# Two-layer streaming encoder on one core: another order for the first units of the frames' attention, both copies of summed outputs on ScalarE, and two layers joined without a barrier

## The chip, the core and the metric

The kernel runs on one core of one Trainium2 chip. The metric is device time in microseconds (us). A profiled execution gives a trace as well, with a span from its first to its last instruction. The engines are TensorE (PE, matmuls; its weight loads are PEld), VectorE (DVE), ScalarE (ACT), GpSimd (POOL) and SyncE (SP, which issues DMA transfers). Each engine works through its own list of instructions in order. The lists meet only in semaphores: a `wait_ge` holds the engine, and all that stands behind it on that engine, until another engine has counted a semaphore up.

## The reference: what is computed

1168 tokens (1024 prompt frames, 8 sample streams of 16 tokens, 16 meta tokens) pass through an input LayerNorm and two layers of

```
z = h @ w_in                                    # to latents, rotary key, window q, k, v
q, q_lat, q_rope, ckv, kr, sq, sk, sv           # RMS norms, rotary embeddings
o_lat = softmax(q_lat @ ckv' + q_rope @ kr') @ ckv        # 8 heads over latents, chunk causal
o_swa = softmax([sq @ sk', sink])[:-1] @ sv               # 8 heads over a window, learned sinks
x   = layer_norm(ALPHA * h + rms(o_lat @ w_uv, o_swa) @ w_out)
h   = layer_norm(ALPHA * x + (silu(x @ wg) * (x @ wu)) @ wd)
```

The outputs are h after layer 2, and each layer's new keys and values. All of it is float32; the kernel splits every operand into a high and a low part and multiplies three times, so that each product is three matmuls (lines 2403 to 2405).

## The kernel before

A layer has four phases. **A** (lines 2411 to 2494 on PE) takes the ten tiles of 128 tokens one by one: transpose the tile (`x_T`), multiply by `w_in` in three blocks (`z`), normalise and rotate on DVE, transpose keys and queries (`post`). **B** (line 2500 on) is the attention of the prompt's frames. **C** is the sample streams and the output projection. **D** is the feed-forward part, with its down projection, the transposes back (`y_T`) and the closing LayerNorm.

Between A and B, between B and C, and between the end of D and the next layer's A stands `barrier` (line 551): each of the five engines drains, counts `phase_done` up and waits for all five. `phase_no` numbers them.

**B's order is a list, `FRAMES`.** `plan_frames` (line 130) writes it, and PE, ACT and DVE each run through the same list, doing their part of each unit (`frames_pe`, `frames_hi`, `frames_lo`). The units are: `wk` turns the key weights; `kn` makes a pair of heads' keys, `vh` its values, `qn` its queries; `qr` makes the rotary queries of four tiles (s = 0 or 1), on DVE six products and a sum; `qs` and `qt` split and turn them; `sx` finds a window tile's score maxima (DVE `tensor_reduce` L2051), `sc` and `sm` turn those into a shift; `mx`, `mc`, `mt` do the same for the latent scores. Then `st` is one step of transposed scores, whose exponential ACT takes (L1558), `sp` splits the exponentials (DVE L2080 and L2084 for the even head, POOL L1262 for the odd), `pv` multiplies by the values into two banks of sums. A pass is a window tile (two steps) or four tiles of latent attention (five or nine). After a pass's last `pv`, `ox` copies the two banks of sums to `oT`: the even head on ACT (L1565), the odd on DVE (L2091). PE waits for both at the first `pv` of the next pass, since the banks are written anew, and at `ot`, which turns `oT`.

A unit's PSUM comes from a ring of three slots of two banks: unit i may start on PE only when unit i-3 of the ring has been read by ACT and DVE (`free_slot`).

Before B's first units DVE waits for ten small loads (`params`, line 1956), among them the meta values of `VB`; PE's keys of `kn` need DVE's `wukNl` behind that wait.

**The joint of the layers.** At D's end PE turns ten tiles back (`y_T`), DVE takes each one's statistics and its first product (`last_stats`, L2369), POOL the root, ACT and POOL or DVE the rest (`last_norm`, L2377 on DVE for tiles 7 and 9), POOL stores it. The next layer's `w_in` is split meanwhile: rows 5 to 7 early, rows 0 to 4 late, ACT making the high and DVE the low part (L608), all five of DVE's behind its last `last_norm`. Then the barrier; then PE turns tiles 0 and 1 (`x_T`, L2420), and starts `z`.

## Time and profile before

| | us |
|---|---|
| runs | 3321.43, 3327.38, 3342.14 (median 3327.38) |
| profiled execution, own time | 3323.12 |
| its span | 3320.8 |
| PE busy | 3074.2 (93%) |
| DVE / ACT / POOL busy | 1526.8 / 869.8 / 832.9 |
| mean granted TensorE clock | 0.959 of full speed |

Busy shares are of the span, and averages over phases with different limits. In a timeline row the number in brackets is how long the engine stood idle before the instruction, and what ended that. Phase B runs from about 201 to 540 us in layer 0 and from about 1845 to 2185 us in layer 1; the layers meet at about 1659 to 1681 us.

### The profile page before, as it was taken

The page shows a single profiled execution, that of the slowest core. Times are in us where ns is not written, and L with a number is a line of the kernel's source. Part 1 is how long each engine was busy: PE and PEld are TensorE (multiplying, and loading weights), DVE is VectorE, ACT ScalarE, POOL GpSimd, SP SyncE. Part 2 cuts the span into 40 slices and gives each one's busy share as a digit, 9 for nine tenths or more (in the row PEclk, how much of TensorE's full clock was granted, in tenths as well). Part 3 has the DMA queues.
Part 4 walks back from the last instruction along what each step waited for, and adds up shares of the span by engine and source line. Part 5 has one row for each costly group of instructions (what it writes and reads, how often), then busy time and mean ns, then how long its engine had stood idle before and what let it go on. Part 6 is the DMA issues. An engine that isn't in the chain of part 4 may idle for free. (4 is left out here: it accounts for less than half of the span.)

```text
span 3320.8 us, 46210 instructions
## 1 busy us (share of the span) xinstructions
PE 3074.2 (93%) x18240; PEld 2791.8 (84%) x18240; DVE 1526.8 (46%) x2883; ACT 869.8 (26%) x1678; POOL 832.9 (25%) x680
## 2 busy tenths in 40 slices
PE   7968888998999999999879788889999999999997
PEld 6956666877999999999879566668789999999996
DVE  6757777653222222222544677776532222222225
ACT  3333334435111111111223233344441111111111
POOL 2323333431212121111422233334212121111113
PEclk9989998999999999999989898989999999999998
DMA  4321104533111111110222211055331111111101
GB/s 161 129 78 34 33 23 153 167 124 110 45 38 42 40 44 38 38 38 25 109 97 98 69 33 33 23 159 178 110 110 42 41 43 39 38 38 38 38 25 71
DMA packets 129041, 231.68 MB, mean 70 GB/s; under 512 B 37744, under 2 KB 78960, under 8 KB 128592
## 3 DMA queue, kind: packets, MB, share of 16 engines
q1 hardware_dynamic: 118336, 198.80, 18.3%
q0 software_dynamic: 10576, 31.14, 2.4%
q8 instruction: 83, 1.36, 0.2%
q14 instruction: 46, 0.38, 0.0%
HBM read 175.46 MB, written 50.38 MB: 68 GB/s over the span
## 5 line engine op out<-in xcount | busy, mean ns | idle before, releaser
L2403 PE MATMUL PS<-xh,fwh 128*128 128x390 f32 (+1 forms) x2112 | 718.8, 340 | 2.0 <-DVE fwl L2309 1.4
L2404 PE MATMUL PS<-xl,fwh 128*128 128x390 f32 (+1 forms) x2112 | 720.0, 341 | 0.0
L2405 PE MATMUL PS<-xh,fwl 128*128 128x390 f32 (+1 forms) x2112 | 718.9, 340 | 0.0
L2351 DVE TENSOR_TENSOR acc<-acc,PS 128x390 f32<-128x390 f32 (+1 forms) x432 | 241.9, 560 | 420.6 <-PE PS L2405 420.6
L2329 DVE TENSOR_TENSOR gate<-PS,gate 128x390 f32<-128x390 f32 x132 | 74.4, 564 | 738.2 <-PE PS L2405 736.9
L2403 PEld LDWEIGHTS PS<-xh,fwh 128*128 128x128 f32 x2112 | 397.9, 188 | 5.1 <-DVE xl L2249 2.6
L2404 PEld LDWEIGHTS PS<-xl,fwh 128*128 128x128 f32 x2112 | 397.3, 188 | 0.4
L2405 PEld LDWEIGHTS PS<-xh,fwl 128*128 128x128 f32 x2112 | 397.3, 188 | 0.0
L2403 PE MATMUL PS<-hidh,fwh 128*128 128x390 f32 (+1 forms) x1056 | 359.5, 340 | 5.2 <-DVE hidl L2333 4.5
L2405 PE MATMUL PS<-hidh,fwl 128*128 128x390 f32 (+1 forms) x1056 | 360.8, 342 | 0.0
L2404 PE MATMUL PS<-hidl,fwh 128*128 128x390 f32 (+1 forms) x1056 | 359.4, 340 | 0.0
L1317 POOL TENSOR_TENSOR fwl<-raw,fwh 128x1024 fp32r<-128x1024 f32 x82 | 195.8, 2398 | 544.5 <-ACT fwh L1757 447.1
L1262 POOL TENSOR_TENSOR Pl<-Pf,Ph 128x256 fp32r<-128x256 f32 (+5 forms) x174 | 219.3, 1267 | 446.1 <-DVE Ph L2080 446.1
L1745 ACT ACTIVATE hidh<-gate 128x390 fp32r<-128x390 f32 x132 | 70.0, 531 | 989.3 <-DVE gate L2329 989.3
L1317 POOL TENSOR_TENSOR fwl<-fraw,fwh 128x1024 fp32r<-128x1024 f32 x42 | 100.4, 2391 | 773.6 <-ACT fwh L1762 673.2
L1558 ACT ACTIVATE Pf<-PS 128x512 f32<-128x512 f32 (+5 forms) x174 | 127.5, 751 | 321.1 <-PE PS L2509 320.8
L2403 PEld LDWEIGHTS PS<-hidh,fwh 128*128 128x128 f32 x1056 | 199.2, 189 | 6.4 <-issue 5.0
L2405 PEld LDWEIGHTS PS<-hidh,fwl 128*128 128x128 f32 x1056 | 200.2, 190 | 0.0
L2404 PEld LDWEIGHTS PS<-hidl,fwh 128*128 128x128 f32 x1056 | 199.0, 188 | 0.0
L2403 PE MATMUL PS<-winh,xTh 128*128 128x394 f32 (+3 forms) x480 | 171.4, 357 | 6.2 <-DVE xTl L1823 3.2
L2404 PE MATMUL PS<-winl,xTh 128*128 128x394 f32 (+3 forms) x480 | 167.5, 349 | 0.0
L2405 PE MATMUL PS<-winh,xTl 128*128 128x394 f32 (+3 forms) x480 | 167.0, 348 | 0.0
(441 smaller groups left out, 5421.1 us busy)
## 6 DMA issues: line engine op xcount, KB each, us to landing
raw<-in_W_FF SPq DMA_DIRECT2D x88, 512.0 KB, 3.2
fraw<-in_W_FF SPq DMA_DIRECT2D x44, 512.0 KB, 3.2
sqt_scratch<-sqTs POOLq DMA_DIRECT2D x18, 512.0 KB, 4.2
hc<-out_H SPq DMA_DIRECT2D x18, 512.0 KB, 3.5
out_H<-yo POOLq DMA_DIRECT2D x18, 512.0 KB, 3.0
dkraw<-in_CKVT SPq DMA_DIRECT2D x16, 520.0 KB, 4.5
QS<-sqt_scratch SPq DMA_DIRECT2D x16, 512.0 KB, 3.4
mt<-mix_scratch SPq DMA_DIRECT2D x16, 512.0 KB, 4.6
```

Of the source, the lines that this page charges most:

```text
L1262: ins = pool.tensor_tensor(Pl[i][0:kk, 1, c], Pf[i][0:kk, 1, c], f(Ph[i][0:kk, 1, c]), ALU.subtract)
L1317: pool.tensor_tensor(fwl[dst][:, :, :], fraw[slot], f(fwh[dst][:, :, :]), ALU.subtract)\
L1558: ins = act.activation(Pf[r][0:kk, :, c], both_banks(u)[0:kk, :, c], ACT.Exp)
L1745: act.activation(hidh[c][:, N0[i]:N0[i] + NT[i]], gate[:, N0[i]:N0[i] + NT[i]], ACT.Copy)\
L2329: dve.tensor_tensor(g, u_bank(i), g, ALU.mult).then_inc(S("f_hid"), 1)
L2351: dve.tensor_tensor(a, a, Tb[e % 2][:, 0:NT[i]], ALU.add).then_inc(S("f_y"), 1)
L2403: pe.matmul(out, wh, mh, start=start, stop=False)
L2404: pe.matmul(out, wh, ml, start=False, stop=False)
L2405: return pe.matmul(out, wl, mh, start=False, stop=stop)
```

## The change

Four things are changed. First, the opening units of `FRAMES`: the rotary queries of the first half only, then the keys, then the window maxima, both window steps `st` of tile 0, only then the five latent maxima, and the rotary queries of the second half behind them. DVE makes `wukNl` ahead of its wait for the small loads. Second, ACT copies both banks in `ox`; DVE copies none; one semaphore takes the place of two. Third, the barrier at the end of D goes (the last one stays); in its place are a wait of PE's first transpose for DVE's last read of PSUM, one of POOL for the down projection, one of SP for the split weights. DVE's last `last_norm` and three of its five late splits move behind the new layer's first `xTl`, the other two between the last statistics. Fourth, `z` of layer 1 takes the rows of `w_in` in the order in which they are split and waits for each by itself, and PE turns tile 1 only after two blocks of tile 0.

```diff
     put("wk")
-    for s in range(2):
-        put("qr", s=s)
-    for kind, more in merged(0):
-        put(kind, **more)
-    for n in (0, 1):
-        put("st", **{k: v for k, v in steps[n].items() if k != "kind"})
+    put("qr", s=0)
+    for kind, more in keys + some("qn") + tile[:5] + some("qs") + tile[5:] + some("qt"):
+        put(kind, **more)
+    first(0)
+    first(1)
+    for kind, more in maxima:
+        put(kind, **more)
+    put("qr", s=1)
+    for kind, more in some("vh") + some("mt"):
+        put(kind, **more)
     put("sp", n=0)
...
-                        act.activation(out_turned(x, 0), out_sums(x, 0), ACT.Copy).then_inc(S("b_ox_even"), 1)
+                        for h in range(2):
+                            ins = act.activation(out_turned(x, h), out_sums(x, h), ACT.Copy)
+                        ins.then_inc(S("b_ox"), 1)
...
-                params(dve, (l, "B"))
-                dve.tensor_copy(sinkB[:, :], sinkAll[:, 4:P * 5:NS * 5])
...
                         dve.tensor_tensor(wukNl[:, :], bank_of(u, 0), f(wukNh[:, :]), ALU.subtract).then_inc(S("b_item_lo"), 1)
+                        params(dve, (l, "B"))
+                        dve.tensor_copy(sinkB[:, :], sinkAll[:, 4:P * 5:NS * 5])
...
-                    elif k == "ox":
-                        x = u["x"]
-                        dve.wait_ge(S("b_pv"), F(l, "pv", u["n"]) + 1)
...
-                        dve.tensor_copy(out_turned(x, 1), out_sums(x, 1)).then_inc(S("b_ox_odd"), 1)
...
                 x_lo(0)
+                if l >= 1:
+                    last_norm(l - 1, TILES - 1)
+                    for k in W_ORDER[1][KD - W_LATE + 2:KD]:
+                        w_in_lo(dve, l, k)
...
                     last_stats(t)
+                    if l + 1 < L and t >= TILES - 2:
+                        w_in_lo(dve, l + 1, W_ORDER[1][KD - W_LATE + t - (TILES - 2)])
                     if t - 1 in NORM_DVE:
-                        last_norm(t - 1)
-                last_norm(TILES - 1)
-                for k in late:
-                    w_in_lo(dve, l + 1, k)
-                barrier(dve, phase_no(l, "D"))
+                        last_norm(l, t - 1)
+                if l == L - 1:
+                    last_norm(l, TILES - 1)
+                    barrier(dve, phase_no(l, "D"))
...
                         pe.wait_ge(S(f"ht_in{t % 2}"), 16 * (TILES // 2 * l + t // 2 + 1))
+                        if t == 0:
+                            pe.wait_ge(S("ln_norm"), norms_done(l - 1, TILES - 1))
...
-                    for k in range(KD):
-                        if t == i == 0 and (l == 0 or k == 0):
-                            pe.wait_ge(S("split_lo"), first[l, "A"] + (k + 1 if l == 0 else KD))
+                    for at, k in enumerate(W_ORDER[l]):
+                        if t == i == 0:
+                            pe.wait_ge(S("split_lo"), first[l, "A"] + at + 1)
...
-                barrier(pe, phase_no(l, "D"))
+                if l == L - 1:
+                    barrier(pe, phase_no(l, "D"))
```

What stands in a row on the engines, at the three places that matter. **The joint, on DVE**, from the last full tile's first product (yo) to the new layer's second tile; winl is the low part of w_in, xTl of the turned tile. Before:

```order
L2369 SCALAR_TENSOR_TENSOR yo_276<-PS,mv_281,lnd 128x1024
L2377 SCALAR_TENSOR_TENSOR yo_279<-yo_279,rstd_292,lnd 128x1024
L638 BN_STATS stats_55<-PS 16x6
L639 BN_STATS stats_55<-PS 16x6
L641 BN_AGGR mv_282<-stats_55 16x2
L643 TENSOR_SCALAR veps_286<-mv_282 16x1
L2369 SCALAR_TENSOR_TENSOR yo_277<-PS,mv_282,lnd 16x1024
L2377 SCALAR_TENSOR_TENSOR yo_277<-yo_277,rstd_290,lnd 16x1024
L608 TENSOR_TENSOR winl<-winraw,winh 128x1184 x5
L1823 TENSOR_TENSOR xTl_91<-PS,xTh_89 128x1024
L1823 TENSOR_TENSOR xTl_92<-PS,xTh_90 128x1024
```

The same place in the changed kernel:

```order
L2393 SCALAR_TENSOR_TENSOR yo_276<-PS,mv_281,lnd 128x1024
L620 TENSOR_TENSOR winl<-winraw,winh 128x1184
L1834 SCALAR_TENSOR_TENSOR yo_279<-yo_279,rstd_292,lnd 128x1024
L650 BN_STATS stats_55<-PS 16x6
L651 BN_STATS stats_55<-PS 16x6
L653 BN_AGGR mv_282<-stats_55 16x2
L655 TENSOR_SCALAR veps_286<-mv_282 16x1
L2393 SCALAR_TENSOR_TENSOR yo_277<-PS,mv_282,lnd 16x1024
L620 TENSOR_TENSOR winl<-winraw,winh 128x1184
L1849 TENSOR_TENSOR xTl_91<-PS,xTh_89 128x1024
L1834 SCALAR_TENSOR_TENSOR yo_277<-yo_277,rstd_290,lnd 16x1024
L620 TENSOR_TENSOR winl<-winraw,winh 128x1184 x3
```

Of the five splits one now stands ahead of tile 7's norm and one behind the last product; the new layer's first xTl comes before the last norm and the other three.

**The start of phase B, on DVE**, up to the first split of exponentials (Ph). Before, from the first rotary products (qrt, qr_raw):

```order
L2007 TENSOR_TENSOR qr_raw<-PS,rotQ 128x4x64 x4
L2014 TENSOR_TENSOR qr_raw<-qr_raw,qrt 128x4x4x64
L2004 TENSOR_TENSOR qrt<-PS,rotQ 128x32x16
L2005 TENSOR_TENSOR qrt<-PS,rotQ 128x32x16
L2007 TENSOR_TENSOR qr_raw<-PS,rotQ 128x4x64 x4
L2014 TENSOR_TENSOR qr_raw<-qr_raw,qrt 128x4x4x64
L2051 TENSOR_REDUCE mxs_161<-PS 64x2 x8
L2064 TENSOR_TENSOR mmS<-mxs_161,nsinkB 128x2x4
```

In the changed kernel, from the window maxima on:

```order
L2081 TENSOR_REDUCE mxs_161<-PS 64x2 x8
L2094 TENSOR_TENSOR mmS<-mxs_161,nsinkB 128x2x4
L2099 TENSOR_TENSOR es_165<-mmS,sinkB 128x8
L2053 SCALAR_TENSOR_TENSOR qrs_136<-qr_raw,qrs_134 128x8x32
L2103 CAST SA_152<-PS 1x512
L2057 CAST QR_131<-PS 128x512
L2063 TENSOR_REDUCE mxc_159<-PS 128x2 x5
L2070 TENSOR_REDUCE mm<-mxc_159 128x8
L2034 TENSOR_TENSOR qrt<-PS,rotQ 128x32x16
L2035 TENSOR_TENSOR qrt<-PS,rotQ 128x32x16
L2037 TENSOR_TENSOR qr_raw<-PS,rotQ 128x4x64 x4
L2044 TENSOR_TENSOR qr_raw<-qr_raw,qrt 128x4x4x64
```

The second half's rotary products have moved from ahead of the window maxima (mxs) to behind the latent maxima (mxc).

**The end of a pass, on DVE**, before (one of 32 such places; x counts equal rows):

```order
L2051 TENSOR_REDUCE mxs_161<-PS 64x2 x4
L2080 CAST Ph_140<-Pf_137 16x1024
L2084 TENSOR_TENSOR Pl_143<-Pf_137,Ph_140 16x512
L2091 COPY oT<-PS 66x512
L2064 TENSOR_TENSOR mmS<-mxs_161,nsinkB 128x2x4
```

and on ACT in the changed kernel, around a pass's end:

```order
L1573 ACTIVATE Pf_138<-PS 128x2x256
L1573 ACTIVATE Pf_138<-PS 80x2x256
L1581 ACTIVATE oT<-PS 66x512 x2
L1573 ACTIVATE Pf_139<-PS 16x1024
L1573 ACTIVATE Pf_137<-PS 128x1024
```

DVE's copy of oT is gone from its list; ACT has two in a row, ahead of the next step's exponential.

## Rows read from the trace of the kernel before

**Rows 1.** The page's first section: busy time, share, instructions.

```profile
PE 3074.2 (93%) x18240; PEld 2791.8 (84%) x18240; DVE 1526.8 (46%) x2883; ACT 869.8 (26%) x1678; POOL 832.9 (25%) x680
```

**Rows 2.** Stretch, length; busy PE, PEld, DVE, ACT, POOL (x); clock, DMA share, GB/s.

```profile
206.10:235.90 29.80, 21.11 (x158) 17.78 (x156) 22.71 (x46) 7.41 (x15) 1.09 (x6) 0.83 0.33 101
245.00:540.00 295.00, 259.38 (x1914) 180.83 (x1914) 228.85 (x387) 96.22 (x157) 106.86 (x84) 0.94 0.10 30
```

**Rows 3.** Waits of PE, 245 to 539 us: total, times, longest.

```profile
PE PS L2403 <- DVE oT L2091: 10.9, 7, 2.8
PE PS L2403 <- DVE Pl L2084: 6.5, 12, 1.5
```

**Rows 4.** Timeline of the joint: start, duration, engine, instruction, idle before.

```profile
1657.07 1.86 PE L2950 MATMUL PS<-ident,acc 128*16 128x128 f32 x8 [0.88 <-DVE yo L2369]
...
1658.96 0.83 SPq L926 DMA_DIRECT2D ht<-out_H  x2
...
1661.26 1.28 DVE L2377 SCALAR_TENSOR_TENSOR yo<-yo,rstd,lnd 128x1024 f32<-128x1024 f32 x1 [1.51 <-POOL yo L1340]
...
1664.07 1.26 DVE L2369 SCALAR_TENSOR_TENSOR yo<-PS,mv,lnd 16x1024 f32<-16x1024 f32 x1
1664.11 3.33 ACT L603 ACTIVATE winh<-winraw 128x1184 fp32r<-128x1184 f32 x3
...
1668.35 6.58 DVE L608 TENSOR_TENSOR winl<-winraw,winh 128x1184 fp32r<-128x1184 f32 x5
...
1675.04 1.97 PE L2420 MATMUL PS<-ident,ht 128*128 128x128 f32 x8 [16.10 <-DVEq L551]
...
1677.10 1.02 ACT L1377 ACTIVATE xTh<-PS 128x1024 fp32r<-128x1024 f32 x1 [9.66 <-PE PS L2420]
1678.23 1.22 DVE L1823 TENSOR_TENSOR xTl<-PS,xTh 128x1024 fp32r<-128x1024 f32 x1 [3.30 <-ACT xTh L1377]
...
1679.60 1.94 PE L2420 MATMUL PS<-ident,ht 128*128 128x128 f32 x8 [2.59 <-DVE xTl L1823]
```

**Rows 5.** Granted clock where layer 1's first projections begin.

```profile
1679.50:1684.00 4.50, 4.40 (x17) 4.43 (x18) 1.23 (x1) 1.02 (x1) 0.00 (x0) 0.51 0.09 34
```

**Rows 6.** Who waited for DVE's copy L2091, both layers.

```profile
  PE PS L2403: 21.9, 14
```

**Rows 7.** Timeline around the ends of passes.

```profile
267.43 0.31 PE L2403 MATMUL PS<-Ph,VN 128*66 128x256 f32 x1 [0.57 <-DVE oT L2091]
...
273.77 0.59 ACT L1565 ACTIVATE oT<-PS 66x512 f32<-66x512 f32 x1 [2.34 <-PE PS L2405]
...
275.14 1.02 ACT L1558 ACTIVATE Pf<-PS 128x1024 f32<-128x1024 f32 x1 [0.77 <-PE PS L2509]
...
276.36 0.68 DVE L2084 TENSOR_TENSOR Pl<-Pf,Ph 16x512 fp32r<-16x512 f32 x1
276.40 1.76 POOL L1262 TENSOR_TENSOR Pl<-Pf,Ph 16x512 fp32r<-16x512 f32 x1 [3.77 <-DVE Ph L2080]
...
277.07 0.69 DVE L2091 COPY oT<-PS 66x512 f32<-66x512 f32 x1
...
277.86 0.66 PE L2403 MATMUL PS<-Ph,VHh 16*66 16x512 f32 x1 [2.76 <-DVE oT L2091]
...
317.19 0.41 PE L2509 MATMUL PS<-KSh,QS 64*128 64x320 f32 x2 [0.73 <-DVE mxs L2051]
...
328.04 0.60 ACT L1537 ACTIVATE QR<-PS 128x512 fp32r<-128x512 f32 x1 [0.17 <-PE PS L2564]
```

**Rows 8.** Granted clock behind such a wait (0.50: of full speed).

```profile
277.80:284.20 6.40, 6.34 (x25) 3.88 (x26) 2.30 (x6) 1.84 (x4) 2.15 (x2) 0.50 0.07 16
```

**Rows 9.** Timeline of the frames' start on DVE and PE, layer 0.

```profile
206.11 0.17 DVE L1957 COPY sinkB<-sinkAll 128x8 f32<-128x8 f32 x1 [5.33 <-DMA VB<-vs_scratch]
...
214.11 0.50 PE L2509 MATMUL PS<-KSh,QS 64*128 64x160 f32 x2 [2.46 <-DVE qr_raw L2007]
...
233.99 0.42 DVE L2080 CAST Ph<-Pf 80x512 fp32r<-80x512 f32 x1
...
235.88 5.41 DVE L2051 TENSOR_REDUCE mxs<-PS 64x2 f32<-64x480 f32 x8 [1.01 <-PE PS L2509]
```

More of the change, by code:

```diff
@@ L177, in merged, with first @@
         return w[:5] + m[:2] + w[5:] + m[2:]
+    def first(n):
+        put("st", **{k: v for k, v in steps[n].items() if k != "kind"})
+    tile, latent = tile_items(0), pass_items(0)
+    keys = [item for item in latent if item[0] == "kn"]
+    maxima = [item for item in latent if item[0] in ("mx", "mc")]
+    some = lambda kind: [item for item in latent if item[0] == kind]
     put("wk")
-    for s in range(2):
-        put("qr", s=s)
-    for kind, more in merged(0):
+    put("qr", s=0)
+    for kind, more in keys + some("qn") + tile[:5] + some("qs") + tile[5:] + some("qt"):
         put(kind, **more)
-    for n in (0, 1):
-        put("st", **{k: v for k, v in steps[n].items() if k != "kind"})
+    first(0)
[5 more added lines that the diff above has]
+        put(kind, **more)
     put("sp", n=0)
@@ L554, in phase_no @@
         def phase_no(l, which):
-            return 1 + 3 * l + "ABD".index(which)
+            return 1 + 2 * l + "ABD".index(which)
         def split_items(l, which):
@@ L946, in _ @@
                         sp.wait_ge(S(f"yo_out{i}"), yo_done(l - 1, i))
+                    sp.wait_ge(S("f_lo"), W_ITEMS * l)
                 first_loads()
-                if l >= 1:
-                    barrier(sp, phase_no(l - 1, "D"))
                 for t in range(2, TILES):
@@ L1198, in _ @@
             for l in range(L):
+                if l >= 1:
+                    pool.wait_ge(S("f_down"), 24 * TURNS * l)
                 pool.memset(f(krn[:, :, :]), 0.0).then_inc(S("set"), 1)
@@ L1348, in _ @@
                         last_norm(t - 1)
-                barrier(pool, phase_no(l, "D"))
+                if l == L - 1:
+                    barrier(pool, phase_no(l, "D"))
             for t in range(TILES - 4, TILES):
@@ L1800, in _ @@
                             w_in_hi(act, l + 1, k)
-                barrier(act, phase_no(l, "D"))
+                if l == L - 1:
+                    barrier(act, phase_no(l, "D"))
         @block.vector
@@ L1810, in _, with last_norm @@
             dve.memset(lateK[CH:P, 8:9], MASKED).then_inc(S("t_zero"), 1)
+            def last_norm(l, t):
+                r, q = rows(t), qD(l, t)
+                dve.wait_ge(S("ln_out"), q)
+                dve.wait_ge(S("ln_root"), q + 1)
+                dve.wait_ge(S("ln_norm"), norms_done(l, t))
+                dve.scalar_tensor_tensor(out=yo[t % 4][0:r, :], in0=yo[t % 4][0:r, :], scalar=rstd[ln_slot(q)][0:r, 0:1],
+                                         in1=lnd[0:r, D:2 * D], op0=ALU.mult, op1=ALU.add).then_inc(S("ln_out"), 1)
             for l in range(L):
@@ L1932, in _ @@
                 x_lo(0)
+                if l >= 1:
+                    last_norm(l - 1, TILES - 1)
+                    for k in W_ORDER[1][KD - W_LATE + 2:KD]:
+                        w_in_lo(dve, l, k)
                 if l == 0:
@@ L2370, in last_stats @@
                                              in1=lnd[0:r, 0:D], op0=ALU.subtract, op1=ALU.mult).then_inc(S("ln_norm"), 1)
-                def last_norm(t):
-                    r, q = rows(t), qD(l, t)
-                    dve.wait_ge(S("ln_out"), q)
-                    dve.wait_ge(S("ln_root"), q + 1)
-                    dve.wait_ge(S("ln_norm"), norms_done(l, t))
-                    dve.scalar_tensor_tensor(out=yo[t % 4][0:r, :], in0=yo[t % 4][0:r, :], scalar=rstd[ln_slot(q)][0:r, 0:1],
-                                             in1=lnd[0:r, D:2 * D], op0=ALU.mult, op1=ALU.add).then_inc(S("ln_out"), 1)
                 params(dve, (l, "D"))
@@ L2387, in _ @@
                         last_stats(LAST_STATS.index(e))
-                late = W_ORDER[1][KD - W_LATE:KD] if l + 1 < L else []
                 for t in range(len(LAST_STATS), TILES):
                     last_stats(t)
+                    if l + 1 < L and t >= TILES - 2:
+                        w_in_lo(dve, l + 1, W_ORDER[1][KD - W_LATE + t - (TILES - 2)])
                     if t - 1 in NORM_DVE:
-                        last_norm(t - 1)
-                last_norm(TILES - 1)
-                for k in late:
-                    w_in_lo(dve, l + 1, k)
-                barrier(dve, phase_no(l, "D"))
+                        last_norm(l, t - 1)
+                if l == L - 1:
+                    last_norm(l, TILES - 1)
+                    barrier(dve, phase_no(l, "D"))
         @block.tensor
@@ L2485, in _ @@
                 for n in range(TILES + 1):
-                    if n + 1 < TILES and not l == n == 0:
+                    if n + 1 < TILES and n:
                         x_T(n + 1)
@@ L2490, in _ @@
                         z(n, 1)
-                    if l == n == 0:
+                    if n == 0:
                         x_T(1)
@@ L2966, in _ @@
                     y_T(t)
-                barrier(pe, phase_no(l, "D"))
+                if l == L - 1:
+                    barrier(pe, phase_no(l, "D"))
 def kernel(x_prompt, x_sample, cache_mla_ckv, cache_mla_krope, cache_swa_k, cache_swa_v,
```

13 lines of the change are left out of this document (5 added, 8 removed).

## The prediction

> **What bounds the kernel now.** I began with the page's busy times: PE works for 93% of the span [rows 1], so time can only come from the places where it stands idle or runs at half its clock. The stretches show two such places that the change touches. In the frames' attention of layer 0, PE is busy for 259.4 of 295 us at a mean clock of 0.94, DVE for 228.9, ACT for 96.2 [rows 2]: PE bounds, DVE is close behind, ACT has room. The waits of PE there name DVE's copy of summed outputs first, 10.9 us in seven waits, and DVE's split of exponentials next, 6.5 us in twelve [rows 3]. Both layers together lose 21.9 us in 14 waits to the copy [rows 6], so layer 1 repeats layer 0. Then the timeline of the joint: PE ends the last turned tile at 1657.07 + 1.86 = 1658.93 and begins the next layer at 1675.04, 16.1 us later, released by DVE, whose five late splits end at 1668.35 + 6.58 = 1674.93 [rows 4]. The reader should see there a chain of single engines, not of work that lacks an engine.
>
> **The joint.** The barrier made PE wait for all five splits. Now its first transposes wait for tile 0's load, issued at 1658.96, and for DVE's last read of PSUM, which ends at 1664.07 + 1.26 = 1665.33 [rows 4]. The second ends last by far. Does DVE still get there in time? One split now stands ahead of tile 7's norm, where DVE stood idle for 1.51 us before 1661.26; a split is 6.58 / 5 = 1.32 us, so it fits, and costs nothing (without that gap it would cost its 1.3 us). From 1665.33 I carry the latencies of the old chain over: DVE's end to PE's start 0.15 (1678.23 + 1.22 = 1679.45 to 1679.60), transposes to ACT 1677.10 - 1675.04 = 2.06, ACT to DVE 1678.23 - 1677.10 = 1.13, DVE 1.22, and 0.15 to PE again. PE turns tile 0 at 1665.48; ACT would take it at 1667.54, just behind its own three splits, which end at 1664.11 + 3.33 = 1667.44; DVE from 1668.67 to 1669.89, its other split (1.32 from 1665.33) done; PE goes on at 1670.04. Before, it went on at 1679.60 with tile 1's transposes [rows 4]. These are not saved but moved behind 48 matmuls. So the gain is 9.6 us.
>
> Does the new chain run into the weights? Five of eight rows of w_in are split by then. The last three follow the last norm on DVE: 1669.89 + 1.27, then three times 1.32, gives 1672.5, 1673.8 and 1675.1. The projections start at half clock, as before (0.51 over 4.5 us [rows 5]); 17 matmuls took 4.4 us there, so the fifteen of five rows take some 3.9 us, to 1673.9, and the sixth row (1672.5) is there. The sixth and seventh rows then take 0.8 us each at that level: 1674.7 and 1675.5, against 1673.8 and 1675.1. No wait; at worst, were PE at full clock, it would wait for the last row by about 1.5 us. ACT now takes tile 1 ahead of tile 0's first results, which only shifts copies that nobody waits for until the third block is done. POOL, behind its last store, waits for DVE's late norm (1671.2) instead of having it at hand; its two fills for the key stack come long before the keys. SP's queue keeps its transfers and order. Bounds: 7 to 10.5 us. I take **-9.6**.
>
> **The copies.** Sixteen ends of passes in each layer. What one is worth depends on what PE waits for there, and the rows show four patterns.
> - Four latent passes before a window pass: waits of 0.57 [rows 7] and much the same in the others. ACT's first copy was done early, and the second fits before its next exponential. All of the wait goes: 4 x 0.6 = 2.4.
> - Three window passes before a latent one: 2.76, of which the copy is only the end. DVE's split ends at 276.36 + 0.68 = 277.04, its copy at 277.07 + 0.69 = 277.76. ACT copies at 273.77, and stood idle for 0.77 before 275.14, so the second copy (0.59) fits. PE then waits for the split: 0.7 less, 3 x 0.7 = 2.1. POOL's part ends at 276.40 + 1.76 = 278.16 and is wanted only after the even head's three matmuls, so it costs 0.1 at most.
> - Three long latent passes: no wait at the copy, but DVE's maxima start behind it, and PE waits for their slot for 0.73 (317.19) [rows 7]. 3 x 0.5 = 1.5.
> - The rest, five early window passes and one late: no gain. In three, ACT goes from copy to exponential to shift to the turned queries without idling (0.17 before 328.04), and PE waits for these; a copy of 0.5 in that row makes it 0.3 later: 3 x 0.3 = 0.9. At the phase's very end the two copies ran side by side and now run in a row: 0.4.
>
> That is 6.0 - 1.3 = 4.7 a layer, **-9.4** for both. Below, nothing of it reaches PE and ACT's delays stay (+2.6); above, DVE's 16 x 0.69 = 11 us a layer come off one by one, -22. I take the middle, since the rows show PE released by exactly this copy.
>
> Behind each of the 2.8 us waits the clock stands at 0.50 for 6.4 us [rows 8], which costs 3.2 us each time. The change leaves 2.1 us of the wait, so I leave the clock as it is, and price the other case below. The Trainium skill (TensorE: Matmul & The Clock Gate, section "A second HAM failure mode: psum-queue depth-cycling") says that frequent short idle stretches between groups of matmuls already make the clock go back and forth between its levels. By it the 2.1 us would cost as much as the 2.8 did, and the sum stays; by a clock that forgives the shorter wait it would be 19 us less.
>
> **The start of the frames.** From 206.11, when DVE's small loads are in, to the first window maxima of tile 1 at 235.88, DVE works 22.7 of 29.8 us [rows 2, 9]: it is the chain, with 7 us of gaps. The same instructions remain. One (0.6 us) moves ahead of 206.11. The second rotary half no longer holds up the window maxima, for which PE waited 2.46 us at 214.11, but it is not gone: its four steps, some 4 us, now stand behind the latent maxima, ahead of the values' split and of the split of exponentials, which began at 233.99 [rows 9]. Replayed with the same durations, DVE is 2.2 us ahead after the window maxima, then waits for the turned queries, the two window steps (whose exponentials must be read before a slot is free) and for PE's new rotary product behind the last maxima. With PE at full clock I come out 1 us ahead at the first split, with PE at half clock there 2 us behind; the stretch before had 0.83 in the mean. I take **+0.5** a layer, +1.0.
>
> **The sum.** 3323.1 - 9.6 - 9.4 + 1.0 = 3305.1 against the profiled execution. The median of the runs was 3327.4, 4 us above that execution, the lowest 3321.4; a median may come out a little above the sum, so I say 3306.
>
> **The rivals.**
> - *The clock comes back.* If waits of 2.1 us no longer send PE to half its clock, six stretches of 3.2 us go as well: 3305 - 19 = 3286. For it: idle time falls all over the phase. Against: 2.1 us is still three quarters of the wait, and the mean is only 0.94 with gaps of all sizes. 0.13.
> - *The copies save nothing.* PE's wait passes on to POOL's split, which ends 0.4 us after DVE's copy did (278.16 against 277.76), or to ACT, and only the joint pays: 3323.1 - 9.6 + 2.6 + 1 = 3317. For it: twelve waits on the split exist already. Against: the odd head's part is wanted 1.3 us later. 0.15.
> - *The joint pays half.* Tile 0's load, the splits or a wait of ACT's come last there, and 4 to 5 us are saved: 3310. 0.07.
> - *Slower than before.* ACT's second copy stands ahead of the next exponential at each of 32 ends. If ACT has no slack there, exponential, split and values all come one copy later: 32 x 0.6 = 19 instead of -9.4, so 3323.1 - 9.6 + 19 + 1 = 3334. It decides where ACT's idle time before its next work is under 0.5 us. At two of the ends in rows 7 it is 0.77 and 0.17, and ACT is busy for a third of the phase, so this holds for few. 0.04.
> - The forecast as summed: 0.61.
>
> Within 1% of 3327.4 is 3294 to 3361, about what a measurement of this kernel can tell from no change. Only the clock's rival lies below that, with a little of the forecast's edge: 0.14 for faster. No case reaches 3361; 0.03 for what I don't see. 0.83 for the same. The range runs from 3289, half way into the clock's rival, to 3321, over the case without a gain from the copies: it leaves out half of the first rival, the slower one and the edges.
>
> **What would show it.** At the joint, PE idle for about 6.5 us instead of 16.1, then its first projection some 11 us after the last turned tile. In the frames, no PE wait on a copy by DVE, PE's 2.8 us waits at 2.1 and put down to DVE's split, 0.5 clock behind them, DVE busy 11 us less in each phase. At the start, the first split of exponentials within 2 us of where it was, counted from the barrier. The prediction is wrong if PE waits on `oT` by ACT in more than a few places, if the clock in the frames rises clearly above 0.94, or if the start differs by more than 2 us.

## The result, and the profile after

The changed kernel takes 3295.39 us (median of four runs, 3293.61 to 3298.02), the kernel before 3329.06 us beside it (3321.43 to 3342.14): a ratio of 0.9896, 95% interval [0.9868, 0.9923]. The forecast was 3306, with 3289 to 3321 around it. The time lies in the range, but the gain is 34 us by the medians where 18 were forecast by the sum. The two profiled executions differ by 29.5 us; the other 4 us are that the median of before lies 6 us above its profiled execution (3323.12), against which the sum was made, and that of the changed kernel 2 us above its own (3293.61).

The first view is again the page's busy times, the answer to [rows 1]:

```profile
span 3291.3 us, 46148 instructions
PE 3065.5 (93%) x18240; PEld 2784.7 (85%) x18240; DVE 1510.1 (46%) x2851; ACT 884.7 (27%) x1710; POOL 834.8 (25%) x680
```

PE has the same 18240 matmuls, and is busy for 8.7 us less. The reader should stop at that: the same matmuls in less busy time point at a higher clock, and the granted clock in the windows below is where to look. I then cut both traces at the same five instructions of PE (the first transpose of the key weights in each layer, the last of `oT` in each, the last `y_T`) and compared the lengths:

| stretch, us | before | after | difference |
|---|---|---|---|
| start to the frames, layer 0 (code unchanged) | 201.26 | 197.27 | -4.0 |
| frames' attention, layer 0 | 338.43 | 331.90 | -6.5 |
| streams, feed-forward, to the last y_T (unchanged) | 1117.38 | 1118.96 | +1.6 |
| last y_T to the frames of layer 1 (the joint) | 188.12 | 180.02 | -8.1 |
| frames' attention, layer 1 | 339.46 | 329.20 | -10.3 |
| rest (unchanged) | 1136.15 | 1133.95 | -2.2 |

The unchanged stretches move by 1.6 to 4 us: what one pair of traces says of a stretch is good to a few us, which is why the experiments have several traces.

**The joint**, in the timeline (start, duration, engine, instruction, idle before), the answer to [rows 4]:

```profile
1648.13 1.87 PE L2968 MATMUL PS<-ident,acc 128*16 128x128 f32 x8 [0.89 <-DVE yo L2393]
...
1649.98 2.33 POOL L1354 TENSOR_TENSOR yo<-yo,lnd 128x1024 f32<-128x1024 f32 x1
...
1651.16 2.41 DVE L620 TENSOR_TENSOR winl<-winraw,winh 128x1184 fp32r<-128x1184 f32 x1
...
1653.49 1.27 DVE L1834 SCALAR_TENSOR_TENSOR yo<-yo,rstd,lnd 128x1024 f32<-128x1024 f32 x1
...
1656.30 1.26 DVE L2393 SCALAR_TENSOR_TENSOR yo<-PS,mv,lnd 16x1024 f32<-16x1024 f32 x1
...
1657.49 1.37 DVE L620 TENSOR_TENSOR winl<-winraw,winh 128x1184 fp32r<-128x1184 f32 x1
...
1657.71 1.94 PE L2440 MATMUL PS<-ident,ht 128*128 128x128 f32 x8 [7.72 <-DVE yo L2393]
...
1662.02 0.70 PE L2420 MATMUL PS<-winh,xTh 128*128 128x396 f32 x1 [2.37 <-DVE xTl L1849]
```

PE stands idle for 7.72 us instead of 16.10, released by DVE's last product as forecast, and begins the projection 13.89 us after the last y_T began. The split that was to fill DVE's gap of 1.51 us took 2.41 us, and the last product ends 9.43 us after PE's last y_T began, not 8.26.

**The frames**: waits of PE in layer 0, 240 to 529.2 us (total, times, longest), the answer to [rows 3]:

```profile
PE PS L2420 <- DVE Pl L2114: 13.9, 17, 2.1
PE PS L2529 <- ACT QR L1555: 4.6, 4, 1.1
PE PS L2529 <- ACT QR L1552: 3.6, 4, 0.9
PE PS L2529 <- ACT Pf L1573: 2.4, 3, 0.8
...
PE PS L2687 <- ACT oT L1581: 1.2, 1, 1.2
```

No wait for a copy by DVE is left, and one for ACT's. The most telling view is that of windows over the frames behind the opening, from the turn of pass 0 to that of pass 15, one row for each layer (columns as in [rows 2]). Length less PE's busy time is PE's idle time, and the busy time of the same matmuls, read beside the granted clock, tells what the clock cost. Before, then after:

```profile
251.74:539.69 287.95, 253.22 (x1866) 176.46 (x1864) 222.44 (x377) 93.20 (x151) 104.41 (x83) 0.93 0.09 28
1894.90:2184.65 289.75, 254.01 (x1865) 176.82 (x1864) 222.44 (x377) 93.09 (x151) 104.39 (x83) 0.94 0.09 28
```

```profile
247.86:529.17 281.31, 251.33 (x1865) 174.62 (x1864) 214.51 (x362) 99.97 (x166) 104.13 (x83) 0.95 0.10 29
1878.76:2157.35 278.59, 248.74 (x1866) 172.88 (x1864) 214.50 (x362) 99.99 (x166) 104.21 (x83) 0.96 0.10 29
```

PE's idle time goes from 34.7 and 35.7 us to 30.0 and 29.9, and its busy time from 253.2 and 254.0 to 251.3 and 248.7. So there are two gains, and only the first had been summed.

### The profile page after: what moved, and what is told of

It reads as the page before. It is cut to its first block and busy times, and to the rows that moved or that the text cites. A ratio compares the mean times of both kernels' runs of the same rounds, so it can differ in the third digit from the quotient of the medians.

```text
span 3291.3 us, 46148 instructions
## 1 busy us (share of the span) xinstructions
PE 3065.5 (93%) x18240; PEld 2784.7 (85%) x18240; DVE 1510.1 (46%) x2851; ACT 884.7 (27%) x1710; POOL 834.8 (25%) x680
```

## The experiments

Each ratio is to the kernel before, run on the same chip in the same rounds, with its 95% interval. Three theories stood at the start: the parts are worth what was forecast, and the rest is chance (**sum**); the copies bring the clock back by making the 2.8 us waits shorter (**A**); the small waits together keep the clock low, wherever they are (**B**).

### The three parts apart, and the whole again

`e1_copies` is the kernel before with this alone (DVE's branch for `ox` goes, and PE waits for one semaphore):

```diff
-                        act.activation(out_turned(x, 0), out_sums(x, 0), ACT.Copy).then_inc(S("b_ox_even"), 1)
+                        for h in range(2):
+                            ins = act.activation(out_turned(x, h), out_sums(x, h), ACT.Copy)
+                        ins.then_inc(S("b_ox"), 1)
```

`e2_start` is the kernel before with the new opening of `FRAMES` and `wukNl` ahead of `params`; `e3_joint` the changed kernel with these two and the copies undone; `a1_all` the changed kernel once more.

> The kernel before with one part alone: ACT copies both banks of sums. Theory A (the frames' gain is the copies'): each layer's stretch from the turned key weights to the last turned sums falls from 338.4 and 339.5 us to some 331 and 330, as in the changed kernel, so the time falls by 14 to 17 us, ratio 0.9955 (0.9945 to 0.9965). PE waits for no copy by DVE; the six 2.8 us waits become 2.1. Theory B (the copies' own sum of 9.4 us is right and the rest of the frames' gain came from the new start): -9 us, ratio 0.9972. Theory C (the copies only pass the wait on): within 2 us of before.

> The kernel before with one part alone: the new order of the first units of the frames, and DVE's key weights ahead of its wait for the small loads. Theory A: the distance from the turned key weights to tile 1's window maxima on DVE stays at 34.6 us in layer 0 and about 34 in layer 1, and the whole time stays within 2 us, ratio 0.9995 to 1.0005. Theory B: the start sets the clock and the rings for what follows, and the frames are 6 to 8 us shorter in the two layers together, ratio 0.998.

> The kernel before with one part alone: no barrier between the layers, late splits moved, weights awaited row by row. Theory A: PE's pause from the last turned tile to its next work falls from 22.5 to 13.9 us, -8.6 us, ratio 0.9974 (0.9969 to 0.9979), and nothing else changes. Rival: the joint also gives back or takes time later in layer 1's projections (the changed kernel spent 0.5 us more there), ratio 0.9985, or the barrier's absence is worth more than the pause, 0.995.

> The changed kernel again, beside its three parts on one chip. If the parts add up: about the product of the three ratios, 0.992 to 0.993 (-25 us), and the 0.9896 measured first holds some luck (the first tile's weights came 4 us earlier in its profile, in code that is the same). If the parts help each other: 0.9896 again while the three parts' gains sum to less than 27 us.

| kernel | median, us | ratio |
|---|---|---|
| copies alone | 3303.62 | 0.9915 [0.9892, 0.9937] |
| opening alone | 3328.22 | 0.9987 [0.9972, 1.0003] |
| joint alone | 3319.51 | 0.9969 [0.9953, 0.9986] |
| all again | 3296.71 | 0.9896 [0.9874, 0.9917] |

The joint gives 10 us (5 to 16), the opening nothing that can be told from zero, the copies 28 us (21 to 36) where 9.4 were forecast, more than any of that run's theories had. The whole without the joint's share, 0.9896 / 0.9969 = 0.9927, gives 24 us for them. The product of the three ratios is 0.9872 and the whole, measured twice, 0.9896: by the intervals the parts may simply add up. The copies' term is the one that was mis-sized. The copies' windows over the frames behind the opening:

```profile
246.67:525.37 278.70, 248.71 (x1865) 172.79 (x1864) 214.47 (x362) 99.88 (x166) 104.16 (x83) 0.96 0.10 29
1881.88:2160.42 278.54, 248.84 (x1865) 172.95 (x1864) 214.58 (x362) 99.84 (x166) 104.20 (x83) 0.96 0.10 29
```

and those of the joint alone, where the copies are as before:

```profile
247.89:535.80 287.91, 253.09 (x1865) 176.35 (x1864) 222.39 (x377) 93.32 (x151) 104.44 (x83) 0.93 0.10 28
1883.65:2174.23 290.58, 254.84 (x1865) 177.38 (x1864) 222.39 (x377) 93.28 (x151) 104.48 (x83) 0.93 0.09 28
```

PE's idle time: 34.8 and 35.7 us with DVE's copies, 30.0 and 29.7 without: 4.8 and 6.0 less, close to the 4.7 forecast. Its busy time: 4.4 and 6.0 less for the same matmuls, while the mean granted clock goes from 0.93 to 0.96 (the time at half clock from 37.5 and 41.0 us to 23.9 in each layer). Half the gain of the copies is clock, and this doesn't hang on one pair of traces. Behind the opening, the three kernels with all copies on DVE (before, opening alone, joint alone) have 255.8 us of busy time in the mean of their six layers (253.1 to 260.8), the four with all copies on ACT 250.0 in the mean of eight (248.6 to 254.7); idle time is 35.0 and 30.0. (The opening alone shows how a single trace can mislead: its profiled execution took 3335.07 us, 7 above its median, and its frames came out 4 and 9 us longer than before, with more busy time of PE and no more idle time, while the runs show no loss.)

### Which copies bring the clock back

Three kernels, each the kernel before with ACT taking the odd head's copy at some ends only:

```diff
                         act.activation(out_turned(x, 0), out_sums(x, 0), ACT.Copy).then_inc(S("b_ox_even"), 1)
+                        if x in (2, 6, 10):
+                            act.activation(out_turned(x, 1), out_sums(x, 1), ACT.Copy).then_inc(S("b_ox_odd"), 1)
```

and DVE's branch for the others. `f1_window_ends` has it as shown (the 2.8 us waits of [rows 7]); `f2_other_ends` has `x not in (2, 6, 10)`; `g1_copy_back` has `x not in (1, 5, 9, 13)`, so DVE keeps only the copies for which PE waited 0.55 to 0.57 us, and 0.84 at the end of pass 13. In these three PE still waits for two semaphores, with all copies on ACT for one.

> The kernel before, with ACT taking the odd head's copy at the ends of passes 2, 6 and 10 alone (those where PE waited 2.8 us), DVE at all others. In the trace of the kernel with all copies on ACT, PE's idle time in the frames is 7 us a layer less and the time lost to half clock another 7 us behind the opening. Theory A, the shorter waits at these three ends let the clock come back sooner: idle falls only by about 1.2 to 2 us a layer, but the time lost to half clock behind the opening falls from about 19 to 12 us a layer, so the frames get 8 us shorter in each, the kernel 16 to 18 us (ratio 0.9950). Theory B, all small waits together keep the clock low: clock loss stays at 18 to 20 us a layer, the kernel gains 3 us (0.9990).

> The kernel before, with ACT taking the odd copy at all ends but those of passes 2, 6 and 10. PE's idle time should fall by about 3.5 to 5.5 us a layer (waits of 0.57 gone, maxima 0.7 earlier in the long latent passes, 1 to 2 us in the opening). Theory A (the three 2.8 us waits decide the clock): half-clock loss stays near 19 us a layer, frames 4 to 5 us shorter, kernel 9 us (ratio 0.9973). Theory B (all small waits together): the clock comes back here, frames 9 to 11 us shorter, kernel about 20 us (0.9940).

> The kernel before, with ACT taking the odd copy everywhere but at the ends of passes 1, 5, 9 and 13, where DVE keeps it and PE waits 0.57 us about 10 us ahead of the long wait at the next window pass's end. All copies on ACT gave 0.9915; the ends of 2, 6, 10 alone 0.9989; all but these 0.9928. Theory C, what counts is how many short waits lie close together, and the 0.57 ones ahead of the long wait make PE stay at half clock longer: PE's idle time rises by only 2.3 us a layer against all copies on ACT, but the half-clock stretches behind the window ends are 6.4 to 7.2 us long again, loss to half clock behind the opening near 18 us a layer instead of 12, ratio 0.995 to 0.996. Rival D, a copy is worth its idle time and the clock follows in proportion: ratio 0.993.

| ACT takes the odd copy | ratio | PE idle, us, layers 0, 1 | PE busy, us |
|---|---|---|---|
| nowhere (before) | 1 | 34.7, 35.7 | 253.2, 254.0 |
| at 2, 6, 10 | 0.9989 [0.9974, 1.0004] | 31.9, 32.4 | 261.3, 258.1 |
| all but 2, 6, 10 | 0.9928 [0.9904, 0.9952] | 31.1, 31.0 | 253.0, 253.4 |
| all but 1, 5, 9, 13 | 0.9973 [0.9957, 0.9988] | 31.4, 31.2 | 252.7, 257.6 |
| everywhere | 0.9915 [0.9892, 0.9937] | 30.0, 29.7 | 248.7, 248.8 |

The windows of the first and the third of these kernels:

```profile
247.63:540.76 293.13, 261.25 (x1865) 181.64 (x1864) 222.65 (x374) 94.76 (x154) 104.46 (x83) 0.91 0.09 28
1899.44:2189.96 290.52, 258.14 (x1865) 179.48 (x1864) 222.71 (x374) 94.86 (x154) 104.48 (x83) 0.92 0.10 28
```

```profile
252.85:536.91 284.06, 252.70 (x1865) 175.99 (x1864) 218.06 (x366) 98.04 (x162) 102.72 (x82) 0.94 0.10 29
1895.74:2184.51 288.77, 257.60 (x1865) 179.16 (x1864) 215.60 (x366) 98.15 (x162) 103.86 (x83) 0.92 0.09 28
```

Theory A falls. At these three ends the wait went from 2.8 to 2.1 us as forecast, 3 us of idle time were saved in each layer, and the kernel gained 4 us (between -1 and 9): PE's busy time rose by 8 and 4 us in the profiled execution. The other ends carry 24 us; 4 and 24 make up the 28 of all ends, so the second semaphore costs nothing that the runs can tell. And B is too even-handed: leaving DVE only the four copies with the shortest waits brings back 1.4 us of idle time a layer, but costs (0.9973 - 0.9915) x 3332 = 19 us of the 28 (10 to 28, by the two intervals). Rival D of that run (0.993) is out as well. C had the direction, with too small a size (0.995 to 0.996), but not the place: the long half-clock stretches that it foretold behind the window ends did not come (below). In that trace PE is busy 13 us longer behind the two openings than with all copies on ACT, and another 5 us in them, ahead of every copy that differs.

What the clock does behind a long wait can be read by cutting the 6.4 us of [rows 8] in two halves. First the kernel with the three ends alone, layer 0, the last of the three; then with all copies on ACT, the same place:

```profile
439.99:443.19 3.20, 3.20 (x8) 1.59 (x10) 2.21 (x4) 0.82 (x3) 0.98 (x1) 0.50 0.23 51
443.19:446.39 3.20, 3.20 (x19) 2.25 (x18) 0.76 (x2) 1.02 (x1) 1.78 (x1) 0.50 0.00 0
```

```profile
429.55:432.75 3.20, 3.02 (x14) 1.71 (x16) 2.21 (x4) 0.82 (x3) 1.00 (x1) 0.86 0.20 43
432.75:435.95 3.20, 3.20 (x17) 2.33 (x16) 1.77 (x5) 1.02 (x1) 1.78 (x1) 0.61 0.01 3
```

The wait ahead is 2.1 us in both. It is tempting to say that the short wait of 0.57 us some 10 us earlier, still there in the first, holds the clock down. The other traces don't bear that out. With four short waits left to DVE, such a wait stands ahead of the first end too, and the clock there is as with all copies on ACT:

```profile
280.04:283.24 3.20, 3.03 (x14) 1.68 (x16) 2.21 (x4) 0.82 (x3) 0.99 (x1) 0.84 0.48 127
283.24:286.44 3.20, 3.20 (x19) 2.32 (x16) 1.70 (x5) 1.02 (x1) 1.77 (x1) 0.63 0.00 0
```

And with all copies on ACT, the second end of layer 0 stands at 0.50 in both halves. The changed kernel's own layers differ as much: 0.50 and 0.50 behind all three ends in layer 0, as in [rows 8], and 0.82 to 0.86, then 0.61 to 0.65, in layer 1. Its first end in each:

```profile
275.14:278.34 3.20, 3.20 (x8) 1.59 (x10) 2.20 (x4) 0.82 (x3) 0.98 (x1) 0.50 0.39 91
278.34:281.54 3.20, 3.20 (x19) 2.26 (x18) 0.77 (x2) 1.02 (x1) 1.78 (x1) 0.50 0.00 0
...
1904.71:1907.91 3.20, 3.03 (x12) 1.68 (x14) 2.21 (x4) 0.82 (x3) 0.99 (x1) 0.82 0.25 56
1907.91:1911.11 3.20, 3.20 (x19) 2.37 (x16) 1.59 (x5) 1.02 (x1) 1.78 (x1) 0.65 0.00 0
```

So one place in one trace says little. Added up from the granted clock of each trace, the time at half clock behind the opening, us a layer (range over the layers), in the passes 2, 6 and 10, which hold the long waits, and in the others:

| ACT takes the odd copy | long wait, us | passes 2, 6, 10 | the others |
|---|---|---|---|
| nowhere (3 kernels, 6 layers) | 2.8 | 20.5 to 27.3 | 13.6 to 30.5 |
| at 2, 6, 10 | 2.1 | 20.5, 20.5 | 34.1, 27.3 |
| all but 2, 6, 10 | 2.8 | 13.7, 13.7 | 21.6, 22.1 |
| all but 1, 5, 9, 13 | 2.1 | 13.7, 17.1 | 19.1, 27.3 |
| everywhere (4 kernels, 8 layers) | 2.1 | 10.2 to 20.5 | 3.4 to 20.5 |

With the long waits shortened alone, 20.5 us stay behind them; with the other copies off DVE it is 13.7, though the long waits are 2.8 us as before. Each of these two is one trace of two layers, and the ranges of the first and last row overlap at their ends, so this is a direction and not a price.

The Trainium skill (TensorE: Matmul & The Clock Gate, section "A second HAM failure mode: psum-queue depth-cycling") says that frequent short idle stretches between groups of matmuls make the clock swing between its levels. The runs agree with it in kind: taking four short waits a layer away (5.0 us in both layers) was worth some four times the idle time they held. Why one set of ends pays and another doesn't is not settled by these runs; the profiled execution of `f2_other_ends` was the slowest of its six (3324.87 against a median of 3309.33), so its windows undersell it.

### The changed kernel with the old opening

`f3_no_start` keeps joint and copies and puts the first units of `FRAMES`, and `wukNl` behind `params`, back.

> The changed kernel with the opening of the frames put back to the old order (joint and copies stay). If the new opening costs what the product of the parts says (0.9896 against 0.9915 x 0.9969 = 0.9884), this one stands at 0.9884 of the kernel before, 4 us faster than the changed kernel; if the forecast of +0.5 us a layer is right, 1 us faster, 0.9893. If the opening helps, 0.991. In the trace the frames should be 328 us in each layer, as with the copies alone (328.3, 328.1), against 331.9 and 329.2 in the changed kernel.

Measured: 3301.73 us, 0.9905 [0.9879, 0.9932]; frames of 328.5 and 330.3 us, against 331.9 and 329.2 in the changed kernel and 336.2 and 331.2 in its repeat. The first split of exponentials comes 31.8 to 32.1 us behind the first key transpose with the old opening, here and with the copies alone, and 32.5 to 32.8 with the new one: the traces put the new opening at a loss of about 0.7 us a layer there, the runs at nothing that can be told. Forecast +0.5 a layer.

### What is left: the waits for DVE's split

In the changed kernel PE waits 14 us a layer for `Pl` by DVE. `e4_split_first` moves the unit `sp` in the list:

```diff
+        if n + 1 < len(steps):
+            put("sp", n=n + 1)
         for kind, more in fills[n]:
             put(kind, **more)
-        if n + 1 < len(steps):
-            put("sp", n=n + 1)
```

`g2_hybrid` does so only where step n + 1 is a window step or the first of a latent pass. `g3_hybrid_plus` is that with the old opening and a moved split at the joint (below), and `h1_first_latent` is `g3_hybrid_plus` with `sp` ahead only at the first step of a latent pass.

> The changed kernel with each step's split of exponentials (sp) ahead of the other units of its place in the list, on DVE. PE's waits for DVE's split (13.8 us in 17 waits in each layer's frames, 2.1 us the longest) should shrink, since splits no longer stand behind maxima. Theory A (PE's long waits for the split are what is left, and bring half the clock): idle falls by 6 to 10 us a layer, half-clock stretches behind the three ends go, kernel 15 to 25 us faster than the changed one, ratio 0.983. Rival: the maxima, now behind, hold PE's slots longer, so that the waits move to mxs and mxc by DVE: same to 10 us slower, 0.990 to 0.993.

> The changed kernel with the split of exponentials ahead of the other units only where the step is a window step or the first of a latent pass; inside latent passes the order stays. With the split ahead everywhere the ratio was 0.985; PE's idle time at the window ends went from 2.4 to 0, but rose from 2.65 to 4.7 in each long latent pass (a wait of 2.85 us on window maxima by DVE), with half-clock stretches behind it. If the two are separate, idle falls by 9 us a layer against the changed kernel and the new stretches go: ratio 0.980 to 0.982. Rival: the gain and the cost hang together, since later maxima of one pass push the next: 0.985 to 0.988.

> The run before (g3: old opening, moved split at the joint) with the split of exponentials ahead of the other units only at the first step of a latent pass, not at window steps. There the waits at the window ends were gone (2.4 us each, now 0), and the new ones of 2.2 to 2.7 us (on window maxima and on QR by DVE, at the ends of the latent passes) come, by the order, from the window steps' splits. If so, PE idles 0 at the ends of passes 2, 6, 10 and 14 and 2.65 in each long latent pass, as with copies alone; frames 31 us of idle a layer instead of 41, about 320 us long instead of 331, kernel 20 us below g3: ratio 0.983. Rival: the latent passes' waits come from the first latent split as well (it delays the maxima behind it): then about 0.989, no gain on g3.

| kernel | median, us | ratio |
|---|---|---|
| `sp` ahead everywhere | 3284.32 | 0.9850 [0.9823, 0.9877] |
| at window steps and first latent | 3296.65 | 0.9891 [0.9871, 0.9911] |
| that, old opening, moved split | 3297.33 | 0.9894 [0.9875, 0.9913] |
| at first latent only, the rest as in the row above | 3321.20 | 0.9972 [0.9960, 0.9984] |

The first beats both kernels: 11 us below the changed one by the medians, 15 by the ratios, whose intervals just overlap. Its windows, and its waits in layer 0:

```profile
252.10:525.38 273.28, 248.35 (x1866) 178.07 (x1864) 207.97 (x360) 100.30 (x166) 102.81 (x82) 0.93 0.10 30
1876.86:2150.16 273.30, 248.13 (x1866) 177.86 (x1864) 208.00 (x360) 100.30 (x166) 102.81 (x82) 0.93 0.10 30
```

```profile
PE PS L2529 <- DVE mxs L2081: 8.5, 3, 2.9
PE PS L2529 <- DVE QR L2073: 8.4, 7, 1.6
```

Idle time is 25 us a layer instead of 30, PE's waits for the split are gone, and new ones on window maxima and turned queries stand there: less than was expected (0.983). By the list of waits, 13.9 us for the split, 4.6 for ACT's `QR` and 3.2 of smaller ones are gone; the two rows above and 1.3 us more, 18.2 in all, came in their place. The half clock moved with the long waits: none stands in the passes 2, 6 and 10 any more, and 20.5 us a layer stand in the long latent passes, which had none in the changed kernel. Behind the first of the new waits:

```profile
312.86:316.06 3.20, 3.20 (x14) 2.72 (x14) 3.11 (x5) 0.00 (x0) 0.00 (x0) 0.50 0.02 5
```

So in these traces half the clock does stand behind a long wait, and the same holds for all six of the new ones. The two measures also part here: the mean clock is 0.93, as in the kernel before, but PE is busy for 248 us instead of 253. Busy time is not the clock alone; what else is in it stays open.

My two refinements both failed, and neither came out as its own rival had it: the hybrid at 0.9891 where 0.980 to 0.982, or 0.985 to 0.988, had been expected, and the last one at 0.9972 instead of 0.983 or 0.989. The hybrid got the three 2.7 us waits on maxima all the same, and 2.2 us on `QR`:

```profile
PE PS L2532 <- DVE QR L2076: 9.0, 4, 2.3
PE PS L2532 <- DVE mxs L2084: 8.0, 3, 2.7
PE PS L2423 <- DVE Pl L2117: 4.9, 6, 1.4
```

and with only the first latent split ahead, the work behind it is late at once, spread over many small waits:

```profile
PE PS L2411 <- DVE Pl L2105: 7.2, 12, 1.5
PE PS L2520 <- ACT QR L1546: 4.5, 4, 1.1
PE PS L2575 <- DVE QNl L2008: 4.5, 3, 1.5
PE PS L2520 <- DVE mixP L2132: 3.7, 3, 1.3
```

```profile
248.86:539.29 290.43, 259.47 (x1865) 180.04 (x1864) 214.83 (x362) 99.84 (x166) 103.87 (x83) 0.91 0.09 28
```

That last row, of the same kernel, is the clock's lesson again. The same window in `g3_hybrid_plus`:

```profile
249.52:528.36 278.84, 248.62 (x1866) 176.14 (x1864) 212.84 (x362) 101.06 (x166) 104.84 (x83) 0.94 0.10 29
```

Idle 30.2 us there and 31.0 here, but busy 248.6 and 259.5, with 34 us at half clock there and 51 here. With the opening's 1.7 us, the idle time says 2.5 us a layer; the runs say 24 us in all.

### The split at the joint

`g3_hybrid_plus` also takes DVE's split from between POOL's product of tile 8 and the norm of tile 7, and puts it behind the new layer's first `xTl` (four there instead of three):

```diff
-                    if l + 1 < L and t >= TILES - 2:
-                        w_in_lo(dve, l + 1, W_ORDER[1][KD - W_LATE + t - (TILES - 2)])
+                    if l + 1 < L and t == TILES - 1:
+                        w_in_lo(dve, l + 1, W_ORDER[1][KD - W_LATE])
```

> As the run before, with the frames' old opening, and at the joint DVE's split of w_in that ran beside POOL's product (2.41 us there, 2.83 to 2.85 in the repeats, against 1.33 to 1.37 for one by itself) moved behind the turned tile's low part. At the joint: DVE's last product ends 8.3 us after PE's last y_T begins (now 9.4), PE turns tile 0 after 8.4 us (now 9.6), no new wait for w_in's last row over 0.5 us. If POOL's product isn't the cause, it stays at 9.4 less one split, or more. In all 1 us from the joint and 0 to 4 us from the opening: 0.979 to 0.982.

Its timeline at the joint:

```profile
1646.91 1.86 PE L2959 MATMUL PS<-ident,acc 128*16 128x128 f32 x8 [0.88 <-DVE yo L2384]
...
1651.12 1.28 DVE L1825 SCALAR_TENSOR_TENSOR yo<-yo,rstd,lnd 128x1024 f32<-128x1024 f32 x1 [1.53 <-POOL yo L1345]
...
1653.94 1.26 DVE L2384 SCALAR_TENSOR_TENSOR yo<-PS,mv,lnd 16x1024 f32<-16x1024 f32 x1
...
1655.35 1.51 PE L2431 MATMUL PS<-ident,ht 128*128 128x128 f32 x6 [6.57 <-DVE yo L2384]
```

The product ends 8.29 us after the last y_T began, PE turns tile 0 after 8.44 us, as expected, and as the forecast had it for the changed kernel (8.41). So the split there cost 1.1 us. The 1 us is too small to be seen in the runs.

## Why the prediction held, and where it was wrong

**The joint: right in its mechanism, 1 us too large.** Forecast -9.6. PE goes on 13.89 us after the last y_T began instead of 22.53, so -8.6 in the trace, and last y_T to the frames is 188.0 to 188.7 us in the traces with the barrier and 178.9 to 180.5 in those without. The step that failed is "DVE stood idle for 1.51 us before 1661.26; a split is 1.32 us, so it fits, and costs nothing". The gap was there for a reason that holds the split too: POOL's product was running, and DVE's split came to its end only 1.26 us after that had ended (1652.31 to 1653.57). The prediction named the price if it didn't fit, 1.3 us; it was 1.1. Everything behind it (the latencies carried over, the second split, no wait over 0.5 us for the last rows of `w_in`) came as replayed: 4.31 us from PE's turn to its projection, 4.56 forecast.

**The copies: the idle time was right, the sum was not.** Forecast -9.4, measured -24 to -28. The waits went as listed: the 0.57 ones away (one of the four was 0.84), the 2.76 ones to 2.08 (275.14, released by DVE's split), long latent passes 0.6 shorter, one wait of 1.2 on ACT's copies; in all 4.8 and 6.0 us of idle time a layer behind the opening. The costs on ACT (1.3 a layer) did not show. The step that failed is "so I leave the clock as it is". Behind the opening PE's matmuls took 4.4 and 6.0 us less a layer in the trace with the copies alone, together 10.4; of the runs' 24 to 28 us, 10.8 are idle time behind the opening and 3.5 in it (12.4 and 11.6 us with the joint alone, 10.2 and 10.3 with the copies alone), which leaves as much or a little more for the clock. The rival "the clock comes back" had the right part of the machine at 0.13, but for a reason that the first of the partial kernels refutes: it hung on the three long waits, which pay 4 us, while four waits of half a microsecond, priced at 2.4 us a layer, pay 19 us. I had read the low clock off one place, behind the first 2.8 us wait (at three of the six the first half stands at 0.62 to 0.63, not 0.50), and taken the length of that wait for all of its cause. A good half of the half-clock time that went did stand there, but it went with the other copies.

**The opening: within its bounds.** Forecast +0.5 a layer. The first split of exponentials comes at 32.49 and 32.79 us behind the first key transpose, before at 32.73 and 31.95, so 0.2 earlier and 0.8 later; against kernels with the same copies and the old opening it is 0.7 later. The first window maxima of tile 1 come at 34.69 and 34.63, before at 34.62 and 33.83. All of it is within the 2 us that were set.

**The other signs.** DVE was to be busy 11 us less in each phase; behind the opening it is 7.9 less, for 15 copies that took 10.2. The missing 2 us are nearly all in one small instruction (below). The clock in the frames came out at 0.95 and 0.96, which the prediction had set as what would show it wrong ("clearly above 0.94"). The slower rival, ACT's second copy ahead of exponentials, did not come: ACT's copies hold PE for 1.2 us in one place of each layer, the phase's very end.

The median of before against its profiled execution was taken as +4 us and is +6 to +9 here (3329 to 3332). Forecast and result differ by 10.6 us: 16 too little gain, which is the copies (15 to 19 too little) less the 1 us of the joint, and 5 us the other way, because the level of before had been set too low. That the time still lies in the range is in part luck: the range reached down half way to a rival whose stated reason did not hold.

## What to carry to other kernels

Where PE bounds, read two numbers from each stretch, its idle time and the busy time of a fixed number of matmuls; a change that removes small waits can pay in the second, several times what it saves in the first, and one that adds them can lose as much. Half clock stands behind long waits and moves with them, but its length isn't set by them alone: here shortening the long waits by a quarter paid 4 us, and taking the copies at the other ends off DVE 24. Try both before you price either, and don't read it off one place of one trace. And before filling another engine's idle gap, ask what the gap was waiting for: if it is an instruction that holds a shared resource, the filler waits too.

## What the runs showed of the hardware

**DVE's operations with two inputs in SBUF are held up beside POOL's.** At the joint the split (winraw, winh) took 2.41 us in the changed kernel and 2.83 to 2.85 in five further traces, beside POOL's product of 2.33 us, and ended 1.3 us behind it each time; the same split beside no product took 1.37. In the frames the same shows in a tiny instruction of 128x8 elements, which joins window maxima and sinks, both in SBUF (timeline, changed kernel):

```profile
274.36 1.76 POOL L1276 TENSOR_TENSOR Pl<-Pf,Ph 16x512 fp32r<-16x512 f32 x1 [3.76 <-DVE Ph L2110]
274.92 1.23 DVE L2094 TENSOR_TENSOR mmS<-mxs,nsinkB 128x8 fp32r<-128x8 f32 x1
```

Alone it takes 0.17 us. Here it ends at 276.15, with POOL's split at 276.12. Its mean over the six in the frames, before and after (groups: count, busy, mean ns):

```profile
L2064 DVE TENSOR_TENSOR mmS<-mxs,nsinkB 128x8 fp32r<-128x8 f32 x6 | 2.1, 342 | 0.0
```

```profile
L2094 DVE TENSOR_TENSOR mmS<-mxs,nsinkB 128x8 fp32r<-128x8 f32 x6 | 4.2, 697 | 0.0
```

Three of the six went from 0.52 to 1.23 us, the others stayed at 0.17. DVE's copy had stood between the two and read PSUM, and POOL did not disturb it (0.69 us beside POOL's 1.76 in [rows 7]). The Trainium skill (SBUF — State Buffer, section "Who interferes with whom") has it that an operation of VectorE with two SBUF inputs contends with one of GpSimd that reads SBUF, that the lock on the port pair they share is exclusive, and that issue order decides which of them blocks; the traces agree. The other direction may show at the joint: POOL's root for the last tile, 0.57 us in the kernel before, is recorded with 2.83 to 2.84 us where DVE's split follows, though spans on POOL are rough.

**The clock is not the same in the same code.** Behind the opening PE was busy 251.3 and 248.7 us in the two layers of the changed kernel, 254.7 and 248.6 in its repeat. The frames' attention moves by 2 and 4 us from one of these executions to the other with nothing changed.
